# Three residual halves taken to the next product without TensorE, in a two-block fp32 kernel on one core

## Chip, core and metric
One core of one Trainium2 chip runs the whole program as one launch. The metric is device time in microseconds. The kernel before takes 901.46 us (median of 3 runs, 901.18 to 901.63).

## The reference
Batch 1, 256 tokens (two tiles of 128), model width 1024, all in fp32. Two blocks of two layers each follow one another on the same residual stream h:

```python
def first_block(x, p, ...):                # layer 0: gated linear attention, layer 1: differential attention
    for i in range(2):
        h = h + mixer_i(rms_norm(h, norm_mix[i]))
        h = h + swiglu(rms_norm(h, norm_ffn[i]), ffn_w_in[i], ffn_w_out[i])
        gate = jax.nn.sigmoid(rms_norm(h, ple_norm[i]) @ ple_w_gate[i])      # "the gate"
        h = h + gate * (p[i] @ ple_w_proj[i])
def diff_attn_mixer(h, ...):
    q, k, v = split(h @ w_in)              # each 256 x 1024, 8 heads of 2 x 64
    q, k = rope(rms_norm(q) * g_q), rope(rms_norm(k) * g_k)
    lam = exp(sum(lam_q1 * lam_k1)) - exp(sum(lam_q2 * lam_k2)) + lambda_init
    a = softmax(q0 k0 / 8) - lam * softmax(q1 k1 / 8)
    return (rms_norm(a @ v) * (1 - lambda_init)) @ w_out
def second_block(x, ...):                  # a short convolution layer, then block attention
```

Every normalised h is the left side of a large product, so it is needed transposed (features on the partitions), while the residual h is kept with tokens on the partitions.

## The kernel before
**Products.** All weights come as 296 units of 512 KB (256 rows by 512 columns), in the order of use, through a ring of four raw buffers; units are numbered 1 to 296 in program order, and END[tile] is the first unit of a tile. For each unit SP issues the transfer (it waits until VectorE's split of unit n - 3 is done, w_lo), ScalarE copies it rounded (whi, L671, fp32r), VectorE subtracts to get the rest (wlo, L1079), both in a ring of eight, and TensorE runs 12 matmuls of 512 columns (L1801): high by high, high by low and low by high, for two token tiles. A tile of 512 output columns is 4 units (11 for the second feed-forward product, 1 for the projection of p) and gathers in a pair of PSUM banks, 0/1 for even tiles and 2/3 for odd ones.

**Order on the engines.** Every queue is written out by hand. `split_to(end)` on ScalarE and VectorE works through all weight units below `end` before it goes on; AHEAD is 6. In differential attention the lists of DF_ORDER say after which unit step each piece of head work comes: an entry (u, step, arg) on ScalarE is preceded by `split_to(END[DF_IN] + u + 7)`, on VectorE by `split_to(END[DF_IN] + u + 6)`. On TensorE it stands before unit END[DF_IN] + u. The first units are 99 (gate of layer 0, PLE0), 109 (DF_IN), 207 (PLE1), 217 (CV_IN) and 257 (MB_IN).

**How the left sides are made.** Half of h (512 features) becomes ready a tile before the other. There are two ways:
- By TensorE: `h_T(1, version)` waits for the residual, and transposes eight 128x128 blocks into banks 6 and 7 (L1854); ScalarE scales and rounds them (`lhs_hi`, L682), VectorE makes the low part (`lhs_lo`, L1095). The second half goes this way at the gate of both layers (a hook before the tile's second unit) and at differential attention (the step "second", before unit 110).
- By VectorE and transfers: `second_blk` (L1119) transposes 32x32 blocks inside partitions into h_blk, SP writes them to DRAM and reads them back with the blocks in place (`second_blocks`, L499 and L502), `second_hi` (L704) and `second_lo` (L1133) make the two parts. Both feed-forward layers, the convolution and block attention take their second half so, and the gate's own output its first half (`gate_blocks`, L512, L515, L876, L1414). Before a wait SP first issues the weight transfers up to a fixed unit.

Where a second half comes by transfers, `first_tiles` interleaves the first two tiles in the order PAIR_ORDER, so that four units need the first half alone.

**Around the gate.** `ffn` on TensorE does tile 24 (4 units), then tile 25 (the projection of p, 1 unit), then 26 and 27. ScalarE takes the sigmoid of the gate's banks (L867), VectorE multiplies by the projection (L1396) and adds to h (L1400).

**Start of differential attention.** ScalarE squares a tile of q or k (L749, df_sq) and evacuates it (L737, df_tok). VectorE sums the squares (L1460), GpSimd makes the factors (L599), VectorE rotates (`df_rope`, L1484 to L1490) and, for tiles 1 and 2, multiplies by the factor (L1467). TensorE transposes the result (`df_T`, L2100), ScalarE copies it (L906), TensorE makes the scores (L2114). The rotation tables df_rot (L1439 to L1443) and the two sums for lambda are made by VectorE after the feed-forward part of layer 0 has ended, the exponentials of the sums by ScalarE (L948), and lambda by VectorE (L1495, L1497), all before the first split of this stage.

## Time and profile before

| | |
|---|---|
| median of 3 runs | 901.46 us |
| profiled execution | 900.89 us |
| its span, first to last instruction | 898.7 us |
| TensorE busy | 892.9 us, 4364 matmuls |
| VectorE busy | 654.6 us |
| ScalarE busy | 506.1 us |
| GpSimd busy | 63.4 us |
| moved by DMA | 187.47 MB, mean 209 GB/s |
| granted TensorE clock | full in all 40 slices |

The profiled execution's own time is 2.2 us longer than its span: what lies before the first instruction and after the last. A row of the timeline gives start, length, engine, line and operation, output <- inputs, how many instructions were merged, and in brackets how long the engine had been idle and what released it. Line numbers are those of the kernel printed above; `bank` is a PSUM bank.

### The profile page before, as it was taken

The page shows a single profiled execution, that of the slowest core. Times are in us where ns is not written, and L with a number is a line of the kernel's source. Part 1 is how long each engine was busy: PE and PEld are TensorE (multiplying, and loading weights), DVE is VectorE, ACT ScalarE, POOL GpSimd, SP SyncE. Part 2 cuts the span into 40 slices and gives each one's busy share as a digit, 9 for nine tenths or more (in the row PEclk, how much of TensorE's full clock was granted, in tenths as well). Part 3 has the DMA queues.
Part 4 walks back from the last instruction along what each step waited for, and adds up shares of the span by engine and source line. Part 5 has one row for each costly group of instructions (what it writes and reads, how often), then busy time and mean ns, then how long its engine had stood idle before and what let it go on. Part 6 is the DMA issues. An engine that isn't in the chain of part 4 may idle for free.

```text
span 898.7 us, 12238 instructions
## 1 busy us (share of the span) xinstructions
PE 892.9 (99%) x4364; PEld 737.0 (82%) x4364; DVE 654.6 (73%) x997; ACT 506.1 (56%) x820; POOL 63.4 (7%) x75
## 2 busy tenths in 40 slices
PE   9999999999999999999999999999999999999998
PEld 8988888888888888778888888888888888887777
DVE  6985478777735699997787776646679897779764
ACT  6756555444444667688564444435664544587681
POOL 0001000000000003211100000000010000215100
PEclk9999999999999999999999999999999999999999
DMA  7674458766755655424487667746568775656621
GB/s 271 197 240 143 162 189 301 277 242 243 240 194 194 227 199 201 160 97 141 139 284 265 237 239 246 254 142 231 202 220 278 260 253 192 207 200 234 227 70 47
DMA packets 76988, 187.47 MB, mean 209 GB/s; under 512 B 6852, under 2 KB 31812, under 8 KB 76936
## 3 DMA queue, kind: packets, MB, share of 16 engines
q1 hardware_dynamic: 75480, 182.99, 59.6%
q0 software_dynamic: 1024, 3.15, 1.0%
q10 hardware_dynamic: 432, 0.66, 0.2%
q8 instruction: 31, 0.51, 0.2%
q14 instruction: 21, 0.17, 0.1%
HBM read 171.83 MB, written 14.94 MB: 208 GB/s over the span
## 4 chain that ended last, share of the span: by engine, by line
PE 95%; DMA 2%; issue 2%; DVE 1%; POOL 1%; ACT 0%; DVEq 0%; POOLq 0%
PE bank L1801 84%; PE bank L1839 3%; PE bank L1854 1%; PE bank L2114 1%; PE bank L2140 1%; DMA mb_pT<-mb_blocks 1%; DMA mb_blocks<-p_tok 1%; DMA h<-x_dram 0%; PE bank L2224 0%; PE bank L2125 0%; PE bank L2253 0%; PE bank L1961 0%; PE bank L2009 0%; PE bank L2013 0%; PE bank L2100 0%
## 5 line engine op out<-in xcount | busy, mean ns | idle before, releaser
L671 ACT ACTIVATE whi<-raw 128x1024 fp32r<-128x1024 f32 x295 | 306.2, 1060 | 186.3 <-DMA raw<-stream_dram 108.8
L1079 DVE TENSOR_TENSOR wlo<-raw,whi 128x1024 fp32r<-128x1024 f32 x295 | 347.5, 1213 | 55.6 <-ACT whi L671 54.8
L1801 PE MATMUL bank<-whi,x_hi 128*128 128x512 f32 x560 | 152.5, 394 | 0.0
L1801 PE MATMUL bank<-wlo,x_hi 128*128 128x512 f32 x560 | 149.9, 389 | 0.0
L1801 PE MATMUL bank<-whi,x_lo 128*128 128x512 f32 x560 | 149.8, 389 | 0.0
L1801 PEld LDWEIGHTS bank<-wlo,x_hi 128*128 128x128 f32 x560 | 105.1, 188 | 22.3
L1801 PEld LDWEIGHTS bank<-whi,x_lo 128*128 128x128 f32 x560 | 105.1, 188 | 22.0
L1801 PEld LDWEIGHTS bank<-whi,x_hi 128*128 128x128 f32 x560 | 103.4, 188 | 21.7 <-issue 1.2
L1801 PE MATMUL bank<-whi,y_hi 128*128 128x512 f32 x396 | 108.0, 394 | 0.1
L1801 PE MATMUL bank<-wlo,y_hi 128*128 128x512 f32 x396 | 106.0, 390 | 0.0
L1801 PE MATMUL bank<-whi,y_lo 128*128 128x512 f32 x396 | 106.0, 389 | 0.0
L1801 PEld LDWEIGHTS bank<-wlo,y_hi 128*128 128x128 f32 x396 | 74.3, 188 | 15.7
L1801 PEld LDWEIGHTS bank<-whi,y_lo 128*128 128x128 f32 x396 | 74.3, 188 | 15.7
L1801 PEld LDWEIGHTS bank<-whi,y_hi 128*128 128x128 f32 x396 | 72.8, 188 | 16.0 <-issue 0.8
L824 ACT ACTIVATE ffn_silu<-bank,rstd 128x256 f32<-128x256 f32 x44 | 18.4, 471 | 76.8 <-PE bank L1801 76.8
L1303 DVE SCALAR_TENSOR_TENSOR ffn_mid<-bank,rstd,ffn_silu 128x256 f32<-128x256 f32 x44 | 19.3, 479 | 54.0 <-ACT ffn_silu L824 54.0
L1801 PE MATMUL bank<-whi,mid_hi 128*128 128x512 f32 x176 | 47.0, 389 | 0.0
L1801 PE MATMUL bank<-wlo,mid_hi 128*128 128x512 f32 x176 | 47.0, 389 | 0.0
L1801 PE MATMUL bank<-whi,mid_lo 128*128 128x512 f32 x176 | 47.0, 389 | 0.0
L1109 DVE TENSOR_TENSOR h<-h,bank 128x512 f32<-128x512 f32 x22 | 14.1, 683 | 44.7 <-PE bank L1801 44.5
L579 POOL TENSOR_TENSOR ms<-stats 128x2 f32<-128x2 f32 x8 | 4.9, 611 | 577.1 <-ACT junk L718 577.1
L1801 PEld LDWEIGHTS bank<-wlo,mid_hi 128*128 128x128 f32 x176 | 33.0, 188 | 6.9
(251 smaller groups left out, 891.4 us busy)
## 6 DMA issues: line engine op xcount, KB each, us to landing
raw<-stream_dram SPq DMA_DIRECT2D x295, 512.0 KB, 4.6
ffn_blocks<-ffn_blk SPq DMA_DIRECT2D x22, 256.0 KB, 2.0
ffn_land<-ffn_blocks SPq DMA_DIRECT2D x22, 256.0 KB, 3.7
second_blocks<-h_blk SPq DMA_DIRECT2D x8, 256.0 KB, 2.0
h_land<-second_blocks SPq DMA_DIRECT2D x8, 256.0 KB, 3.1
cv_blocks<-cv_blk SPq DMA_DIRECT2D x7, 256.0 KB, 5.2
cv_land<-cv_blocks SPq DMA_DIRECT2D x7, 256.0 KB, 3.3
h_blocks<-h_blk SPq DMA_DIRECT2D x3, 512.0 KB, 6.3
```

The source lines that it names most:

```text
L579: step(nc.gpsimd.tensor_tensor(ms[:, j, 0, :], stats[:, j, 0, :], stats[:, j, 1, :], ALU.add))
L671: A(whi[:, u % RING, :], raw[:, u % RAW, :], ACT.Copy).then_inc(sem("w_hi"), 1)
L824: A(sg[:, (t - tin) % 2, k, :], bank[2 * (t % 2) + k][:, 0:256], ACT.Silu, scale=rstd[:, j, k:k + 1]).then_inc(sem("ffn_silu"), 1)
L1079: V.tensor_tensor(wlo[:, u % RING, :], raw[:, u % RAW, :], whi[:, u % RING, :].bitcast(F32), ALU.subtract).then_inc(sem("w_lo"), 1)
L1109: V.tensor_tensor(h[:, t, half * HALF:(half + 1) * HALF], h[:, t, half * HALF:(half + 1) * HALF], bank[2 * (tile % 2) + t][:, :], ALU.add) ...
L1303: V.scalar_tensor_tensor(mid[:, (t - tin) % 2, :, k, :], bank[2 * (t % 2) + k][:, 256:512].rearrange("p (k n) -> p k n", k=2), rstd[:, j, ...
L1801: last = T.matmul(bank[pair + t][:, :], lhs[a][:, kt, t * P:(t + 1) * P], w[:, u % RING, kk * NW:(kk + 1) * NW], start=part != 1 and k == ...
L1839: last = T.matmul(bank[pair + hd // 2][:, hd % 2 * SEQ:(hd % 2 + 1) * SEQ], w[:, u % RING, kk * NW + hd * P:kk * NW + (hd + 1) * P], lhs[a ...
L1854: last = T.transpose(bank[b][:, k * SEQ + t * P:k * SEQ + (t + 1) * P], src[:, t, kt * P:(kt + 1) * P], ident)
L2114: last = T.matmul(bank[DF_S_BANKS[hd][m]][:, q * SEQ:(q + 1) * SEQ], dT[r, 0, hd, q * P:(q + 1) * P], dT[r, 1, hd, :], start=True, stop=True)
L2140: last = T.matmul(bank[b][:, q * SEQ + (hd % 2) * P:q * SEQ + (hd % 2 + 1) * P], daT[:, hd % 4, k * SEQ + q * P:k * SEQ + (q + 1) * P], dv ...
```

## The change
1. The second half of h at the gate (both layers) and at differential attention goes by VectorE and transfers; `h_T(1, ...)` is used nowhere.
2. The transfers of `second_blocks` and `gate_blocks` no longer go through DRAM. `cross` issues four of them, each from 32 partitions of h_blk to one quarter of h_land's free dimension.
3. The gate's units run in the order GATE_ORDER: gate, gate, projection, gate, gate. The next gate tile gathers in banks 4 and 5.
4. Differential attention's first two tiles run in PAIR_ORDER, by `first_tiles`; its lists change at the start: ScalarE takes tile 0 at step 6 (was 4), VectorE rotates it at 7 (was 5), TensorE transposes its first half at 11 (was 8).
5. The rotation tables and the two sums for lambda are made in `ffn(0)`, behind the gate's second half; ScalarE's exponential comes before the first Exp of the scores, VectorE's lambda before the first soft step. The tile df_rot lies elsewhere in memory.
6. Counters are named by a list of uses instead of numbers.

```diff
-PAIRED = (FFN_IN0, FFN_IN1, CV_IN, MB_IN)
+PAIRED = (FFN_IN0, DF_IN, FFN_IN1, CV_IN, MB_IN)
+USES = ("mix0", "ple0", "gate0", "df", "mix1", "ple1", "gate1", "cv", "mb")
+GATE_ORDER = ((0, 0), (0, 1), (1, 0), (0, 2), (0, 3))
 DF_ORDER = {
     "pe": (
-        (1, "second", 0), (8, "qkT", 0), (11, "qkT", 1), (12, "qkT", 2), (13, "scores", 0), (13, "qkT", 3),
+        (11, "qkT", 0), (11, "qkT", 1), (12, "qkT", 2), (13, "scores", 0), (13, "qkT", 3),
     "act": (
-        (4, "tile", 0), (8, "tile", 1), (9, "qkT", 0), (12, "qkT", 1), (12, "tile", 2), (12, "qkT", 2),
+        (6, "tile", 0), (8, "tile", 1), (11, "qkT", 0), (11, "qkT", 1), (12, "tile", 2), (12, "qkT", 2),
     "dve": (
-        (5, "rope", 0), (6, "more", 0), (6, "sums", 0), (8, "rope", 1), (8, "sums", 1), (10, "more", 1),
+        (7, "rope", 0), (7, "sums", 0), (8, "more", 0), (8, "rope", 1), (8, "sums", 1), (10, "more", 1),
...
+            def cross(dst, src, signal):
+                for i in range(P // B):
+                    sp.dma_start(dst[:, i, :], src[i * B:(i + 1) * B, :]).then_inc(sem(signal), 16)
             def second_blocks(r, tile):
-                at = END[tile] + (7 if tile == CV_IN else 8)
+                at = END[tile] + (7 if tile in (DF_IN, CV_IN) else 8)
                 fetch(done, at)
                 for q in range(2):
                     sp.wait_ge(sem("g_blk"), 2 * r + q + 1)
-                    sp.dma_start(s_dram[s, q], sblk[:, q, :]).then_inc(sem(f"g_out{q}"), 16)
-                for q in range(2):
-                    sp.wait_ge(sem(f"g_out{q}"), 16 * (r + 1))
-                    sp.dma_start(sland[:, q, :, :], s_dram[s, q]...).then_inc(sem(f"g_land{q}"), 16)
+                    cross(sland[:, q, :, :], sblk[:, q, :], f"g_land{q}")
...
                 done = half_blocks(n, tin + FT)
+                done = second_blocks(use(f"ple{n}"), tin + FT + 2)
                 done = gate_blocks(n, tin + FT + 2)
+                if n == 0:
+                    done = second_blocks(use("df"), DF_IN)
...
# ScalarE, ffn
                 split_to(END[tple] + 1 + AHEAD)
-                lhs_hi(src, norm_gain(j), (6, 7))
                 squares(j, 1)
+                second_hi(j, src, use(f"ple{n}"), END[tple])
                 for half in range(2):
                     t = tple + 2 * half
-                    split_to(END[t + 1] + AHEAD - 2 * half)
-                    c.wait(act, "w_used", END[t + 1])
+                    over = END[t + 1 + (half == 0)]
+                    split_to(over + AHEAD - 1 - half)
+                    c.wait(act, "w_used", over)
...
# VectorE, ffn
                 residual(tout + 1, 1)
-                split_to(END[tout + 2] + 1 + AHEAD)
-                lhs_lo(src, norm_gain(j), (6, 7))
+                second_blk(12 * n + 6)
+                second_lo(j, src, use(f"ple{n}"), END[tple])
+                if n == 0:
+                    df_tables()
...
-                    elif n == 0:
-                        split_to(END[DF_IN] + 1 + AHEAD)
-                        lhs_lo(dst, norm_gain(j + 1), (6, 7))
                     else:
                         second_blk(12 * n + 10)
-                        second_lo(j + 1, dst, 4, END[CV_IN] - 1)
+                        second_lo(j + 1, dst, use("cv" if n else "df"), END[tple + 4] - 1)
...
# TensorE
-                product(tple, src, "ple_sig", need=more2, hooks=[(1, second_half2)])
-                product(tple + 1, PT, "ple_gated", need=[("pT", 2 * (n + 1))])
-                product(tple + 2, src, "ple_sig")
+                more2 = list(half0) + second_need(use(f"ple{n}"))
+                for at, (t, k) in enumerate(GATE_ORDER):
+                    product(tple + t, PT if t else src, "ple_gated" if t else "ple_sig" if k == 3 else None,
+                            need=[("pT", 2 * (n + 1))] if t else more2, only=k, at=END[tple] + at)
+                product(tple + 2, src, "ple_sig", pair=4)
...
-            product(DF_IN, Y, "df_in", need=df_half0, beside=df_beside)
-            for t in range(1, 6):
+            first_tiles(DF_IN, Y, "df_in", list(half) + second_need(use("df")), df_beside)
+            for t in range(2, 6):
                 product(DF_IN + t, Y, "df_in", beside=df_beside)
```

`df_tables` holds the table and sum operations of L1439 to L1451 unchanged, except that the products of the lambda vectors are written to df_m2 and no longer to df_o.

## Rows read from the trace of the kernel before

**Rows 1.** the page, busy shares (part 1) and head of the chain (part 4).
```profile
PE 892.9 (99%) x4364; PEld 737.0 (82%) x4364; DVE 654.6 (73%) x997; ACT 506.1 (56%) x820; POOL 63.4 (7%) x75
...
PE 95%; DMA 2%; issue 2%; DVE 1%; POOL 1%; ACT 0%; DVEq 0%; POOLq 0%
```
**Rows 2.** the chain that ended last, in order of time: start us, us, what.
```profile
117.41 184.98 PE bank L1801 x816
302.39 0.87 PE bank L1854 x8
303.26 27.34 PE bank L1801 x120
330.61 0.90 PE bank L1854 x8
...
362.53 0.28 issue
362.81 0.63 PE bank L2100 x4
...
627.67 116.98 PE bank L1801 x516
```
**Rows 3.** timeline, gate: start us, us, engine, line, operation, tiles, count [idle before <-releaser].
```profile
299.70 1.28 DVE L1109 TENSOR_TENSOR h<-h,bank 128x512 f32<-128x512 f32 x2 [2.73 <-PE bank L1801]
...
311.48 1.27 ACT L867 ACTIVATE ple_gate<-bank,rstd 128x512 f32<-128x512 f32 x2
```
**Rows 4.** timeline, start of the convolution layer: VectorE, ScalarE, SP.
```profile
652.27 1.29 DVE L1396 TENSOR_TENSOR ple_gated<-ple_gate,bank 128x512 f32<-128x512 f32 x2 [1.90 <-PE bank L1801]
...
654.68 2.22 DVE L1119 STREAM_TRANSPOSE h_blk<-h 128x256 f32<-128x256 f32 x4
...
661.32 1.15 DVE L1133 SCALAR_TENSOR_TENSOR x_lo<-h_land,cols,x_hi 128x128 fp32r<-128x128 f32 x4
...
660.57 0.91 ACT L704 ACTIVATE x_hi<-h_land,cols 128x256 fp32r<-128x256 f32 x2 [2.13 <-DMA h_land<-second_blocks]
...
663.96 1.06 ACT L671 ACTIVATE whi<-raw 128x1024 fp32r<-128x1024 f32 x1 [0.39 <-issue]
665.64 1.06 ACT L671 ACTIVATE whi<-raw 128x1024 fp32r<-128x1024 f32 x1 [0.61 <-DMA raw<-stream_dram]
...
659.37 17.23 SPq L438 DMA_DIRECT2D raw<-stream_dram  x9
```
**Rows 5.** all uses of tile h_land: issue of one read (ns), its landing (us).
```profile
L502 SPq DMA_DIRECT2D h_land<-second_blocks x8: 370/371/371, 124.6 to 767.8; - x8
...
DMA to landing us min/median/max: 2.6/3.2/4.9
```
**Rows 6.** all uses of tile h_blk: landing of its writes to DRAM.
```profile
DMA to landing us min/median/max: 2.0/2.0/6.4
```
**Rows 7.** timeline, start of differential attention: VectorE, ScalarE.
```profile
336.39 0.28 DVE L1439 SCALAR_TENSOR_TENSOR df_rot<-consts,rows 128x128 f32<-128x128 f32 x1
...
340.18 4.63 DVE L1079 TENSOR_TENSOR wlo<-raw,whi 128x1024 fp32r<-128x1024 f32 x4 [0.57 <-ACT whi L671]
344.72 0.75 DVE L1484 TENSOR_TENSOR df_m<-df_tok,df_rot 128x256 f32<-128x256 f32 x2
...
361.42 1.29 DVE L1467 TENSOR_TENSOR df_tok<-df_tok,df_ss 128x512 f32<-128x512 f32 x2
...
334.13 1.28 ACT L948 ACT_TABLE_LOAD   x1
...
339.03 3.89 ACT L671 ACTIVATE whi<-raw 128x1024 fp32r<-128x1024 f32 x4
342.82 1.24 ACT L749 ACTIVATE df_sq<-bank,rstd 128x512 f32<-128x512 f32 x2
...
347.28 1.06 ACT L671 ACTIVATE whi<-raw 128x1024 fp32r<-128x1024 f32 x1 [1.11 <-DMA raw<-stream_dram]
```
**Rows 8.** tile raw, 330 to 366 us: issue to landing of blocks.
```profile
DMA to landing us min/median/max: 3.1/4.4/4.8
```

More of the change, by code:

```diff
@@ L431, in _ @@
                     SOURCE[END[tile] + n] = END[tile] + (KT // 2) * t + k
+            for tile in (PLE0, PLE1):
+                for n, (t, k) in enumerate(GATE_ORDER):
+                    SOURCE[END[tile] + n] = END[tile + t] + k
             SOURCE[END[CV_OUT] + 3], SOURCE[END[CV_OUT] + 4] = END[CV_OUT] + 4, END[CV_OUT] + 3
@@ L510, in gate_blocks @@
                 for t in range(TT):
-                    sp.wait_ge(sem("g_blk"), 2 * (2 * n + 1) + t + 1)
-                    sp.dma_start(g_dram[n, t], gblk[:, t, :]).then_inc(sem(f"g_out{t}"), 16)
-                for t in range(TT):
-                    sp.wait_ge(sem(f"g_out{t}"), 16 * (2 * n + 2))
-                    sp.dma_start(gland[:, t, :, :], g_dram[n, t].rearrange("q n -> (q n)")
-                                 .rearrange("(i p w) -> p i w", i=P // B, p=P)).then_inc(sem(f"g_land{t}"), 16)
+                    sp.wait_ge(sem("g_blk"), 2 * use(f"gate{n}") + t + 1)
+                    cross(gland[:, t, :, :], gblk[:, t, :], f"g_land{t}")
                 return max(done, at)
@@ L528, in _ @@
                 done = END[out_tile]
-                done = second_blocks(2 * n, tin)
+                done = second_blocks(use(f"mix{n}"), tin)
                 fetch(done, done_at(tin) + 10)
@@ L550, in _ @@
             done = max(done, END[MB_IN])
-            done = second_blocks(5, MB_IN)
+            done = second_blocks(use("mb"), MB_IN)
             fetch(done, UNITS)
@@ L694, in mixer_lhs @@
                 squares(j, 1)
-                second_hi(j, dst, 2 * (j - 1) // 3, END[out + 4])
+                second_hi(j, dst, use(f"mix{(j - 1) // 3}"), END[out + 4])
             def second_hi(j, dst, r, base):
@@ L729, in next_lhs @@
                 squares(j, 1)
-                second_hi(j, dst, 5, END[first + 1])
+                second_hi(j, dst, use("mb"), END[first + 1])
             def evacuate(tile, j, dst, width, signal, func=ACT.Copy, scale=None):
@@ L955, in _ @@
                 elif step == "scores":
+                    if arg == 0:
+                        act.wait_ge(sem("df_lam"), 2)
+                        A(lam[:, 2:4], lam[:, 0:2], ACT.Exp).then_inc(sem("df_lamexp"), 1)
                     df_exp(arg)
@@ L1753, in product @@
             def product(tile, lhs, signal, kt0=0, need=None, hooks=(), beside=None, part=None,
-                        only=None, at=None, turned=False, inside=None):
-                pair = 2 * (tile % 2)
+                        only=None, at=None, turned=False, inside=None, pair=None):
+                pair = 2 * (tile % 2) if pair is None else pair
                 hooks = dict(hooks)
@@ L2143, in df_av @@
                 last.then_inc(sem("df_av"), 1)
-            df_half0, df_pairs = list(half) + [None, None], [None] * 4
+            df_pairs = [None] * 4
             def df_beside(u):
@@ L2150, in df_beside @@
                         continue
-                    if step == "second":
-                        df_half0[2:4] = h_T(1, 3)
-                    elif step == "qkT":
+                    if step == "qkT":
                         df_T(arg)
```

98 lines of the change are left out of this document (45 added, 53 removed).

## The prediction
> **What bounds the kernel now.** First the page's busy shares and the head of its chain [rows 1]: TensorE is busy 99% of the span and the chain that ended last is TensorE for 95%. So only two things can move the time: matmuls taken out, and new waits of TensorE. Then the chain in order of time [rows 2]. A unit is 12 matmuls of one 512 KB weight block; 184.98 us for 68 units is 2.72 us each, back to back. Three pieces of eight transposes (L1854) stand in that stream before units 100, 110 and 208: 0.87, 0.90 and 0.87 us (the third, at 626.80, repeats the first). These are the second residual halves that the change takes from TensorE. The one wait in this stretch is 0.28 us, before the transposes of head step 2 at 362.81. Third, the other engines around these places: VectorE and ScalarE in the gate [rows 3] and in differential attention [rows 7], and, as a model of what the change puts there, the start of the convolution layer, which already gets its second half by VectorE and transfers [rows 4].
>
> **Removed.** 24 transposes, 0.87 + 0.90 + 0.87 = 2.64 us, all on the path. With nothing added the profiled execution goes from 900.89 us (span 898.7) to 898.25; the median of the runs shown, 901.46, lies 0.57 above the profiled one, and I carry differences over to it: 898.8.
>
> **The gate's second half (twice).** Unit 98 ends at 302.39 - 2.72 = 299.67. With the projection's unit in third place, TensorE wants the second half at unit 102, 3 x 2.72 later, 307.83. VectorE adds the residual 299.70 to 300.98 [rows 3]; four block transposes take 2.2 us, the first pair being ready after 1.15 [rows 4], so SP starts at 302.1 (300.98 + 1.15). It issues four transfers at 0.37 us each [rows 5], the last at 303.2 to 303.5. The trace has no transfer from SBUF to SBUF. Nearest rows: 2.0 us to DRAM in the median (6.4 for the one form of 512 KB) [rows 6], back from it 2.6 to 3.2 and at most 4.9 [rows 5]. With 3.2 the half lands at 306.7, ScalarE scales two tiles in 0.91, 307.6: 0.2 us to spare. With 2.0 there are 1.4 to spare, with 4.9 TensorE waits 1.5 us, twice in the kernel. The lower parts: VectorE does the residual, the transposes (to 303.2), four weight splits (to 307.9), then 1.15 to 309.1; TensorE wants them two thirds into unit 102, 309.6. I take no wait, between ends of 0 and 3.0 for both.
>
> The Trainium skill ("DMA: Bandwidth & Descriptors", Anatomy of one DMA) gives a fixed cost of about 2.0 us, most of it the receipt from the target memory, heaviest for HBM; by it a direct 64 KB transfer lands some 2.15 us after issue, an estimate from that page, and the case with 4.9 has less to speak for it. The trace agrees in that 256 KB go in 2.0 us.
>
> **The tables made earlier.** Twelve small products and the lambda sums, 336.39 to 338.89, 2.5 us of VectorE [rows 7], now come after the gate's second half, at 310.3 to 312.8, then one weight split to 314.0. TensorE ends unit 103 in the new kernel at 299.67 + 5 x 2.72 = 313.3, and ScalarE's first sigmoid (0.63, half of the pair's 1.27 [rows 3]) at 313.95. VectorE is there at the same moment: no cost. Weights are split up to unit 107 by then, four units ahead of TensorE. The gate's first half then lands no later than before (its transfers save a round trip), so unit 109 finds it.
>
> **Differential attention's second half.** Unit 108 ends 0.87 us earlier than before, at 303.26 + 9 x 2.72 - 0.87 = 326.9. The convolution's start has the same structure, and TensorE waits for nothing there [rows 2]; I carry its offsets over [rows 4], counted from the first gated product (652.27 there, 326.9 here). VectorE's transposes end at +4.6 (331.5), four splits (units 112 to 115) at +9.1 (336.0), the lower parts at +11.4 (338.3) if it never waits. TensorE wants the half at unit 113, 337.8, the lower parts at 339.6. No wait here.
>
> **What follows it: the new order of the head steps.** Here I expect the loss. Before, ScalarE evacuates tile 0 after the splits up to unit 119 and VectorE rotates it after them; the new lists put these at steps 6 and 7, after the splits up to unit 121. Those two splits must come first in both queues, and they come round a ring of four raw buffers: VectorE's split n lets SP fetch unit n+4, which lands 4.4 us later in the median (3.1 to 4.8), ScalarE rounds it in 1.06, VectorE subtracts in 1.16 [rows 7, 8].
> - SP has issued the eight direct transfers by 326.9 + 3.6 (the first pair of block transposes) + 8 x 0.37 = 333.5, then fetches 116. In the convolution the first unit after SP was free (659.37) was rounded at +4.6, the next at +6.3 [rows 4]. So unit 116 at 338.1 and 117 at 339.8, VectorE done with them at 340.4 and 342.1 (with the hand-over between the engines). Before the change all four had landed long before they were wanted, because both engines were held by the lambda chain until 339.03 [rows 7].
> - Unit 121's fetch is freed by 117's split: 342.1 + 4.4 = 346.5, rounded at 347.6. Only now does ScalarE take tile 0: squares 1.24, first token half 0.63, rotation can start at 349.4 (before: 344.72, with TensorE 1.8 us later in its stream).
> - Tile 2 wants tile 0's banks at unit 117, 326.9 + 8 x 2.72 = 348.7; they are free at 350.1. That is a new wait of 1.4 us, contained in the next.
> - VectorE from the first rotation to the last unit factor: before 344.72 to 362.71 with five splits (units 120 to 124), 18.0 us without a gap [rows 7]. Now three splits: 18.0 - 2 x 1.16 = 15.7. 349.4 + 15.7 = 365.1, and TensorE's transposes of step 2 at 365.2 instead of 362.81: +2.4.
> From there the order is the old one, and ScalarE's copy behind these transposes is late with them, so TensorE carries +2.4 through the stage. It has already used the two gains of 0.87 and 0.90. The last 0.87 (before unit 208) remains: +2.4 - 0.9 = **+1.5 us**.
>
> Bounds of this term. Low: VectorE goes on at 338.3 and never waits; its nine splits, rotations, sums and factors are 9 x 1.16 + (18.0 - 5 x 1.16) = 22.6 us, ending at 360.9, TensorE's wait is about the old 0.28 and the whole change gives -2.6. With every landing at its minimum of 3.1 us, tile 0 is taken at 345.3 and the step comes at 362.9: -0.8 overall. High: fetches at 4.8 behind each other put tile 0 at 348.5: +2.4.
>
> **Small edits.** The two small lambda operations on VectorE move from before the first split of rows 7 (338.89 to 340.18, mostly waiting) into the first soft step, and the Exp table load of 1.28 us, which ran at 334.13 in a gap [rows 7], comes before the first Exp. Both then stand between the first scores and TensorE's first aT transposes, three units (8.2 us) later by the lists; I take 0, between 0 and the load's 1.3. Layer starts that used DRAM before (four) had no wait and keep none; there the change saves traffic only. The projection's banks: the gate's second tile moves to banks 4 and 5, free for long: 0.
>
> **Rivals.**
> - *Full gain.* Weights land early, VectorE has no gap, the order costs nothing: -2.4 to -2.6 us, 898.9. For it: VectorE is relieved of 2.5 us there. Against: in rows 7 a unit's rounding waits 1.11 us for its landing (two more such waits follow), with the queue fed no worse than it will be.
> - *Short delay.* The same chain with quick landings: between -0.9 and +0.7 us, near 901.3.
> - *The direct transfers are late* (slower for certain): four small transfers and the raw blocks share one queue, landing at 4.9 as the slowest read did. Its place is unit 102 and unit 210; it decides once a landing takes over 3.4 us from the last issue. 2 x 1.5 on top of +1.5 (part of the first is absorbed, since the attention chain starts later by the same): +2.4 to +4.5, 904.6. The Trainium skill ("DMA: Bandwidth & Descriptors", Issuing engines are not separate DMA queues) says that all DMAs run on the same 16 engines and interleave; in the convolution's start a weight block issued at 659.7 was rounded only at 665.64 [rows 4], which agrees.
>
> **How the numbers follow.** The forecast's case (tile 0 taken between 346.8 and 348.5) holds from +0.7 to +2.4 us: 0.42; short delay 0.20; full gain 0.22; late transfers 0.16. A change of under 0.2%, 1.8 us, can't be told from none here. Of the first case a third lies over 1.8 (0.14), so slower is 0.14 + 0.16 = 0.30, faster 0.22, same 0.28 + 0.20 = 0.48. Time of the likeliest: 901.46 + 1.5 = 902.96, given as 902.9. The range holds the full gain nearly whole and half of the late transfers: 898.9 to 904.7; the forecast's own case is 902.2 to 903.9.
>
> **What would show it.** Right: no L1854 pieces before units 100, 110, 208; a wait of TensorE at unit 117 for df_tok (L737) of 1 to 2 us and one before L2100 of 2 to 4; tile 0 squared (L749) at 347 or 348; whi waits for raw ahead of it. Wrong: tile 0 squared by 344, or L2100 without a wait (full gain); a wait of TensorE near 307 to 310 for x_hi or x_lo (late transfers); a wait before aT (the table load is not hidden).

## The result and the profile after

The changed kernel takes 906.54 us (median of 7 runs, 905.33 to 908.03), the kernel before 901.46 (median of 7 on the same chip, 900.16 to 904.4): ratio 1.0058, 95% interval 1.0046 to 1.0069, so 5.1 us slower. The forecast was 902.9, between 898.9 and 904.7: the sign was right, the size was not (slower had been given 0.30). The profiled execution took 905.53 us (span 903.7), before 900.89 (898.7).

The page of the kernel after, busy shares, head of the chain, and the issues of the direct transfers (KB each, us to landing):
```profile
PE 891.9 (99%) x4340; PEld 735.3 (81%) x4340; DVE 663.7 (73%) x1021; ACT 508.1 (56%) x820; POOL 65.7 (7%) x75
...
PE 88%; DVE 4%; DMA 3%; SPq 2%; issue 1%; ACT 1%; ACTq 0%; DVEq 0%
...
h_land<-h_blk SPq DMA_DIRECT2D x72, 64.0 KB, 2.1
```
Against [rows 1]: 24 instructions fewer on TensorE, 24 more on VectorE with 9.1 us of work. TensorE's share of the chain falls from 95 to 88%. That is not the length of its waits, which are 7.4 us in the four lines below and under 1% of the span: where TensorE waits, the chain runs back through VectorE, SP and the transfers that it waited for, while TensorE was still busy. Where it waits, the list of TensorE's waits after says (us in total, times, longest):
```profile
PE bank L1810 <- ACT df_tok L745: 4.5, 1, 4.5
PE bank L2106 <- issue: 1.6, 1, 1.6
...
PE bank L1810 <- ACT x_hi L885: 0.7, 1, 0.7
PE bank L1810 <- ACT y_hi L712: 0.6, 1, 0.6
```
The first two stand in differential attention's start, where [rows 2] had 0.28. Timeline of that stretch after, in turn for SP, ScalarE and VectorE (columns as in rows 3):
```profile
318.72 5.08 SPq L504 DMA_DIRECT2D h_land<-h_blk  x8
...
330.88 5.22 SPq L504 DMA_DIRECT2D h_land<-h_blk  x8
336.50 6.34 SPq L460 DMA_DIRECT2D raw<-stream_dram  x5
...
337.63 0.91 ACT L712 ACTIVATE y_hi<-h_land,cols 128x256 fp32r<-128x256 f32 x2 [1.67 <-DMA h_land<-h_blk]
339.89 1.06 ACT L679 ACTIVATE whi<-raw 128x1024 fp32r<-128x1024 f32 x1 [1.34 <-DMA raw<-stream_dram]
342.51 1.06 ACT L679 ACTIVATE whi<-raw 128x1024 fp32r<-128x1024 f32 x1 [1.56 <-DMA raw<-stream_dram]
344.52 1.06 ACT L679 ACTIVATE whi<-raw 128x1024 fp32r<-128x1024 f32 x1 [0.95 <-DMA raw<-stream_dram]
...
350.34 1.25 ACT L757 ACTIVATE df_sq<-bank,rstd 128x512 f32<-128x512 f32 x2
...
341.08 1.23 DVE L1086 TENSOR_TENSOR wlo<-raw,whi 128x1024 fp32r<-128x1024 f32 x1 [1.76 <-ACT whi L679]
...
352.20 0.76 DVE L1492 TENSOR_TENSOR df_m<-df_tok,df_rot 128x256 f32<-128x256 f32 x2 [0.51 <-ACT df_tok L745]
...
366.64 1.29 DVE L1475 TENSOR_TENSOR df_tok<-df_tok,df_ss 128x512 f32<-128x512 f32 x2
```
SP is in the eight issues from 330.88 to 336.10 and only then fetches unit 116, whose buffer VectorE had freed near 333.0 (the first of its four splits from 331.83). Unit 116 lands 3.4 us after its issue; the three blocks sent close behind it (337.5 to 338.6) take 5.0 to 7.1 us, where [rows 8] had 4.8 at most. Every rounding up to the one before tile 0 waits for its raw block; tile 0 is squared at 350.34, where [rows 7] has 342.82. The same in windows of 4 us (busy us and count of PE, PEld, DVE, ACT, POOL; granted clock; DMA share; GB/s):
```profile
334.00:338.00 4.00, 4.00 (x20) 3.30 (x18) 3.46 (x7) 2.02 (x6) 2.50 (x3) 1.00 0.45 109
338.00:342.00 4.00, 4.00 (x19) 3.34 (x18) 2.06 (x5) 1.60 (x3) 0.00 (x0) 1.00 0.95 306
342.00:346.00 4.00, 4.00 (x20) 3.30 (x19) 1.92 (x3) 2.36 (x3) 0.00 (x0) 1.00 0.82 323
...
352.00:356.00 4.00, 3.16 (x8) 2.51 (x9) 3.73 (x7) 3.50 (x6) 0.90 (x1) 0.59 0.71 267
356.00:360.00 4.00, 4.00 (x19) 3.29 (x18) 3.90 (x8) 3.45 (x5) 2.58 (x2) 0.99 0.41 133
```
The DMA engines are half idle while SP is held, then loaded at 0.95 and 0.82 to refill the ring, and VectorE has 2 us of work in 4. From 352 us on, behind the first rotation, VectorE is full (3.73 and 3.90 of 4). TensorE itself, timeline after:
```profile
347.29 1.07 PE L1810 MATMUL bank<-whi,y_lo 128*128 128x512 f32 x4
352.84 2.04 PE L1810 MATMUL bank<-whi,y_hi 128*128 128x512 f32 x4 [4.49 <-ACT df_tok L745]
354.69 1.74 PE L1810 MATMUL bank<-wlo,y_hi 128*128 128x512 f32 x4
...
357.19 1.09 PE L1810 MATMUL bank<-whi,y_hi 128*128 128x512 f32 x4
...
368.04 0.63 PE L2106 MATMUL bank<-consts,df_tok 128*128 128x128 f32 x4 [1.61 <-issue]
...
371.35 1.14 PE L2120 MATMUL bank<-df_qkT 64*128 64x256 f32 x8
```
Groups of four matmuls that take 1.07 us elsewhere take 2.04 and 1.74 behind the wait, at a granted clock of 0.59 over the window of 4 us, which mixes 1.2 and 2.4 GHz. The next unit comes 4.35 us later (352.84 to 357.19); a unit behind a wait with the clock at 1.00 took 2.84 (e18 below).

Two marks that all kernels share measure the place: the first matmul of unit 99 (the gate) and the first score matmul. Before they are 66.65 us apart (299.50, 366.15), after 72.13 (299.22, 371.35): +5.48. It adds up: waits 4.49 + 1.61 - 0.28, clock 1.51, less two pieces of transposes (0.87 + 0.90) = 5.56. Outside this stretch: -0.28 ahead of it; the third piece gone (-0.87) with waits of 0.6 and 0.7 in the second gate and the convolution's start; waits of 1.1 us in block attention that the trace of before has and this one has not. That makes 4.5 of the span's 5.0; where the other 0.5 lies stays open.

### The profile page after: what moved, and what is told of

The parts are those of the page before. It is cut to its first block, busy times and chain, and to the rows that moved or that the text cites. A ratio compares the mean times of both kernels' runs of the same rounds, so it can differ in the third digit from the quotient of the medians.

```text
span 903.7 us, 12249 instructions
## 1 busy us (share of the span) xinstructions
PE 891.9 (99%) x4340; PEld 735.3 (81%) x4340; DVE 663.7 (73%) x1021; ACT 508.1 (56%) x820; POOL 65.7 (7%) x75
## 4 chain that ended last, share of the span: by engine, by line
PE 88%; DVE 4%; DMA 3%; SPq 2%; issue 1%; ACT 1%; ACTq 0%; DVEq 0%
PE bank L1810 77%; PE bank L1848 3%; DMA raw<-stream_dram 2%; SPq L504 2%; DVE wlo L1086 1%; PE bank L2120 1%; PE bank L1863 1%; PE bank L2146 1%; PE bank L2228 1%; PE bank L2257 1%; PE bank L2131 0%; DVE h_blk L1126 0%; DMA h_land<-h_blk 0%; DVE ple_gated L1431 0%; PE bank L1906 0%
## 5 line engine op out<-in xcount | busy, mean ns | idle before, releaser
L1810 PEld LDWEIGHTS bank<-whi,y_lo 128*128 128x128 f32 x396 | 74.4, 188 | 15.7
L1810 PEld LDWEIGHTS bank<-whi,mid_hi 128*128 128x128 f32 x176 | 33.0, 188 | 6.9
```

Of the source, the lines that this page charges most:

```text
L1810: last = T.matmul(bank[pair + t][:, :], lhs[a][:, kt, t * P:(t + 1) * P], w[:, u % RING, kk * NW:(kk + 1) * NW], start=part != 1 and k == ...
```

## The experiments

"Stage" is the distance between the two marks in the run's one profile; ratios are timed, against the kernel before on the same chip. e7 is not in the table: its kernel is longer by design and ran once (926.45 us).

| run | what it is | ratio [95%] | stage, us (before 66.65) | longest waits of TensorE in it |
|---|---|---|---|---|
| after | the change | 1.0058 [1.0046, 1.0069] | 72.13 | 4.49, 1.61 |
| e1 | through DRAM | 1.0059 [1.0043, 1.0075] | 69.97 | 2.07, 1.54 |
| e2 | old order of head steps | 1.0065 [1.0053, 1.0077] | 73.03 | 0.99, 5.44 |
| e6 | both (the base below) | 1.0054 [1.0041, 1.0067] | 71.65 | 4.59 |
| e14 | attention's half alone, direct | 1.0060 [1.0043, 1.0077] | 71.49 | 2.25, 1.55 |
| e3 | gate's half alone, direct | 1.0013 [1.0002, 1.0023] | 67.52 | 1.44 |
| e8 | gate's half alone, DRAM | 0.9991 [0.9982, 1.0000] | 65.44 | none |
| e17 | e8, tables at the old place | 0.9990 [0.9979, 1.0000] | 65.89 | 0.33 |
| e4 | before, direct transfers | 0.9999 [0.9990, 1.0007] | 66.66 | 0.30 |
| e13 | before, tables early | 1.0011 [1.0002, 1.0020] | 66.89 | 0.47 |
| e9 | after, issued by GpSimd | 1.0133 [1.0118, 1.0149] | 73.40 | 2.96, 1.65 |
| e10 | e9, old order | 1.0096 [1.0081, 1.0110] | 72.95 | 3.45, 1.28 |
| e11 | e6, unit 116 fetched first | 1.0040 [1.0027, 1.0053] | 70.43 | 0.97, 2.88 |
| e12 | e6 less VectorE's lower parts | 1.0056 [1.0043, 1.0069] | 71.77 | 4.43 |
| e15 | e6 less VectorE's transposes | 1.0042 [1.0026, 1.0059] | 71.68 | 4.38 |
| e16 | e6, splits before the half | 1.0076 [1.0055, 1.0098] | 77.48 | 4.60, 2.87 |
| e18 | before + a wait at unit 117 | 1.0037 [1.0024, 1.0050] | 67.07 | 0.66 |
| e19 | before + a longer one | 1.0083 [1.0065, 1.0101] | 71.21 | 3.25 |

**Is it the transfers or the order of the head steps? (e1, e2, e6)** e1 sends the halves through DRAM as before, e2 puts head step "tile 0" back to step 4 and its rotation to 5, e6 does both:
```diff
-                    cross(sland[:, q, :, :], sblk[:, q, :], f"g_land{q}")
+                    sp.dma_start(s_dram[r, q], sblk[:, q, :])...
+                for q in range(2):
+                    sp.wait_ge(sem(f"g_out{q}"), 16 * (r + 1))
+                    sp.dma_start(sland[:, q, :, :], s_dram[r, q]...)
...
-        (6, "tile", 0), (8, "tile", 1), (11, "qkT", 0),
+        (4, "tile", 0), (8, "tile", 1), (11, "qkT", 0),
```


> The changed kernel with its block transfers through DRAM again (one write and one read for each half, as before the change), all else as changed. Theory A (SP's issue): each of the 8 direct transfers costs SP 0.60 us of issue, so SP fetches unit 116 only at 336.5; with the round trip SP is free 3.5 us after the first pair of blocks, at 334.4, 2.1 us earlier. Then tile 0 is taken 2.1 us earlier, TensorE's wait at unit 117 falls from 4.5 to about 2.4 us, the waits at units 210 and 217 (0.6 and 0.7) go, and the time falls by 3.4 to 5 us, to 901.5 to 903. Theory B (the order of the head steps alone): the direct transfers cost nothing, the time stays at 906 within 1 us or rises, since the round trip lands the halves later.

> The changed kernel with the first head steps where they were: ScalarE takes tile 0 at step 4 (was 6), VectorE rotates at 5 and 6 (was 7 and 8); direct transfers kept. Theory A (SP's issue feeds the weights late, the order is second): ScalarE takes tile 0 at 346.8 instead of 350.3, the wait at unit 117 falls from 4.5 to about 1.1 us and TensorE's clock does not fall, but VectorE's chain is still fed late and ends at 366.6 instead of 367.9: 1.3 us faster, 905.2. Theory B (order alone): the whole loss of the attention stage goes, 5 us or more faster, 901 or less.

> The changed kernel with both: block transfers through DRAM and the first head steps where they were. Theory A: SP free 2.1 us earlier and tile 0 taken before the splits of units 120 and 121: VectorE's first rotation at 346.5, its chain ends at 364.5, 3.5 us before the changed kernel's, and the gate's waits go: 901.7, so still no faster than the kernel before. Theory B (order alone): as the early order alone, 901 or less. If the two costs add up fully (2.1 and 5 us): 899.


All three lie at the changed kernel's time (906.3, 906.3 and 906.1 us), so the gains expected by theory A for e1 and e6 and by theory B for e2 and e6 did not come. e2's waits of TensorE:
```profile
PE bank L2106 <- DVE df_tok L1475: 5.4, 1, 5.4
...
PE bank L1810 <- ACT df_tok L745: 1.0, 1, 1.0
```
The order moves the wait and does not make it: the 4.5 us stood at unit 117, now 5.4 stand at step 2. The step that I blamed in the prediction is not the cause. The new order even shields something: with it the slow clock behind the first wait falls into time that TensorE would have spent in the second (step 2 comes at 368.04 and the scores 3.31 us later); in e2 step 2 comes at 367.70 and the scores at 372.68, 4.98 us later. e1's profile has the best stage of the three: SP fetches unit 116 there 35.06 us after unit 99 begins, 37.28 in the changed kernel, and the stage is 2.16 us shorter. Its timed runs do not show it; they reach from 903.7 to 908.8, so that gain is open.

**Which part? (e3, e8, e14, e4, e13, e17)** e3 and e8 undo differential attention's part (TensorE transposes the half, old order) and keep the gate's; e14 undoes the gate's and keeps the other; e4 and e13 put one edit into the kernel before; e17 is e8 with tables and lambda where they were.
```diff
-PAIRED = (FFN_IN0, DF_IN, FFN_IN1, CV_IN, MB_IN)
+PAIRED = (FFN_IN0, FFN_IN1, CV_IN, MB_IN)
...
-                second_hi(j + 1, X if n else Y, use("cv" if n else "df"), END[tple + 4] - 1)
+                if n == 0:
+                    lhs_hi(Y, norm_gain(j + 1), (6, 7))
```


> The changed kernel with differential attention's second half, unit order and lists as before the change (eight transposes on TensorE, no interleaved tiles); the gate's second halves by VectorE and direct transfers, the gate's unit order and the early tables stay. Theory A: the loss sits in the attention stage; here two groups of transposes are gone (1.8 us) against waits of 1.3 us at units 210 and 217: 901.0, the time before within 1 us. Rival (the gate's direct transfers are the larger loss): 903 or more.

> The kernel whose gate alone is changed (two groups of transposes gone, early tables), with its block transfers through DRAM. With direct transfers it took 901.83, with waits of 0.4 and 1.4 us before and behind unit 110. Theory A: SP is held 3.5 us instead of 5.1 at the gate, so the waits shrink by 1 to 1.5 us and the time is 900 to 901, a little under the kernel before. Rival (the gate's second half by VectorE is late by VectorE's and ScalarE's own work, not by SP): 901.8 or more.

> The changed kernel with the gate's part undone (its second half by TensorE's transposes again, its tiles in their old order); differential attention's half, the direct transfers, the new order of head steps and the early tables stay. Theory A (nearly all of the loss is differential attention's half): TensorE loses 16 of the 24 transposes less of work, about 0.9 us gained in place of 2.6, and has the same wait of 4 to 5 us ahead of unit 117 or the scores with the clock at half behind it: 905.5 to 907, ratio 1.0045 to 1.0065. Theory B (the gate's part, by holding SyncE just before, makes half of the loss): 903 to 904.5, ratio 1.002 to 1.0035, and the wait is 2 us shorter.

> The kernel before with one part of the change: the block transfers that it already had (four second halves, two gate outputs) go directly instead of through DRAM, four issues for each pair. Theory A: the weights come later at these places too, but there is slack in the feed-forward and convolution layers; at the gate SP is held 5.1 us instead of 4.1: within 1 us of 901.05. Rival (issue time counts everywhere): 903 or more.

> The kernel before with one part of the change alone: VectorE makes the rotary tables and lambda's sums ahead of the gate's second half, and lambda is finished at its new place; all transposes, transfers and the order of head steps are those of before. VectorE is relieved of some 2 us in the stage that starts differential attention. Theory 1: the wait of 0.28 us at the unit before the scores goes and nothing else changes: 901.0 to 901.3, ratio 0.9990 to 1.0005. Theory 2 (the tables, made while the gate runs, hold the gate's halves): a wait at the gate's second half of the units appears, ratio above 1.001.

> The gate's part alone through DRAM (900.2, ratio 0.9991 when it was run before) and the tables and lambda made at their old place. The tables made early, alone, were at ratio 1.0011. Theory A (tables made early hold the gate's products of VectorE for a little): without them the gate's part gives 0.3 to 1 us more: 899.3 to 900, ratio 0.998 to 0.9985. Theory B (they cost nothing, 1.0011 was the noise of a measurement): 900.2 again, with the 0.28 us wait at the unit before the scores back: ratio 0.9987 to 0.9997.


Differential attention's half alone is the whole loss: e14's ratio is the changed kernel's. Its waits:
```profile
PE bank L1805 <- ACT df_tok L741: 2.2, 1, 2.2
PE bank L2104 <- issue: 1.6, 1, 1.6
```
The gate's half is worth about 0.9 us through DRAM (e8, e17: two runs that agree, though each interval reaches 1.0000). Direct, it is not: e3 and e8 differ by 2.2 in a thousand with intervals apart, though the same transfers at the old places cost nothing (e4). e3 fetches the weights of the next stage from 324.91, e8 from 322.55, and TensorE waits 1.44 us at 335.9. Tables made early are not worth moving: e13 has the 0.28 us wait gone and one of 0.47 at 314.65 in its place, and is 1.1 in a thousand slower; e17 and e8, with the gate's new order, are equal.

**What does the issue cost? (e7, e9, e10)** e7 is the kernel before with groups of transfers behind its end, all queues empty; e9 and e10 let GpSimd issue all direct transfers.
```diff
+            for i in range(4):
+                sp.dma_start(land0[:, i, :], h[i * B:(i + 1) * B, 0, 0:NW])...
+            sp.wait_ge(sem("out_done"), 16 * (5 + 4))
...
+                for i in range(P // B):
+                    nc.gpsimd.dma_start(dst[:, q, i, :], src[i * B:(i + 1) * B, q, :])...
```


> The kernel before with nothing changed but its last microseconds: there SyncE issues, each group waited for before the next, four transfers of 32 x 512 float from SBUF into a tile of 128 x 4 x 128 (the shape of the direct transfers), four of 32 x 512 into the same shape in SBUF, four of 32 x 512 to DRAM, four from DRAM as 128 x 128, and then four single ones of 128 x 512 in SBUF. Theory 1 (the issue pays for how the bytes are laid out on the receiving side): the first group costs 0.55 to 0.60 us per issue as in the changed kernel, the second 0.33 to 0.38. Theory 2 (the issue pays for SBUF on both sides): both cost 0.55 or more, the DRAM ones 0.33 to 0.38. Theory 3 (the issue was long because the queue was full of weights then): all are under 0.4 here, where the queues are empty. The time as a whole is longer by the transfers added at the end (10 to 15 us) and says nothing.

> The changed kernel with all its direct block transfers issued and waited for by GpSimd, which is idle there, each before the row norm of the same place; SP does weight blocks alone. Theory A (SP, held for 3.5 to 5 us by each set of waits and issues, feeds the weights late): SP fetches unit 116 at 333.0, as soon as its buffer is free, instead of 336.5; tile 0 is taken about 3 us earlier, the wait at unit 117 falls from 4.5 to 1 to 1.5 us, TensorE's clock stays up (1.6 us), and the gate's waits go if GpSimd's transfers land in time: 901 to 903. Theory C (VectorE's own work bounds the stage: four block transposes and the later splits; the feed does not matter): 905 to 906.5, with VectorE without gaps from 338 to 366.

> As the kernel with GpSimd's transfers, and the first head steps where they were before the change (tile 0 at step 4, rotation at 5 and 6). Theory A: with both the feed and the order mended VectorE's chain ends at about 362, TensorE waits under 1 us: 899 to 901. Theory C: as the other early orders, 905 to 906.


The lines of e7's groups (issue in ns, min/median/max): SBUF to 128x128 slices, SBUF to the same shape, SBUF to DRAM, DRAM to 128x128, and 128x512 in SBUF:
```profile
L563 SPq DMA_DIRECT2D raw<-h x4: 595/604/696, 899.6 to 901.6; - x4
...
L566 SPq DMA_DIRECT2D raw<-h x4: 591/592/603, 903.7 to 905.6; - x4
...
L569 SPq DMA_DIRECT2D h_blocks<-h x4: 342/420/431, 907.7 to 909.0; - x4
...
L572 SPq DMA_DIRECT2D raw<-h_blocks x4: 588/602/604, 910.7 to 912.6; - x4
...
L576 SPq DMA_DIRECT2D raw<-h x4: 465/484/517, 914.9 to 922.0; - x4
```
0.60 us also with empty queues, so theory 3 falls; the layout at the receiver makes no difference (first against second group), so theory 1 falls; and the fourth group comes from DRAM at 0.60, so theory 2 does not hold as I put it. What is common to the three dear groups is that a quarter of a tile (64 KB) goes to SBUF; the rule behind it stays open. Their landing is 2.0 to 2.5 us. GpSimd is no way out: e9 took 912.6 and e10 910.2 us where 901 to 903 and 899 to 901 were expected. The issues themselves are not late: the eight for this stage take 4.32 us (333.90 to 338.22) and start when VectorE's first pair of transposes is ready. The landings are. The page of e9 (KB each, us to landing), against 2.1 us from SP in the changed kernel's page above:
```profile
h_land<-h_blk POOLq DMA_DIRECT2D x72, 64.0 KB, 3.5
```
In this stage they took 2.0 to 4.6 us (2.1 to 2.3 from SP), at the first gate 2.1 to 4.7. TensorE waits for the halves in both gates (1.65 us at 309.63 in e9), and in the stage ScalarE, which takes the half before the next weights, stands 3.47 us for its second pair. SP was free there and fetched unit 116 at 335.94, as soon as its buffer was, and TensorE still waited 2.96 us at unit 117: freeing SP alone does not help when the half comes late. Whether the landings are long because of GpSimd's issue or because SP's weight blocks are then under way beside them was not tested.

**What makes tile 0 late? (e11, e12, e15, e16)** All from e6. e11 fetches unit 116 between SP's writes and reads of the half; e12 leaves out VectorE's lower parts of that half (2.2 us of work), e15 its four transposes (the transfers carry what was there); e16 has VectorE split two units first and SP fetch two units more before the half.
```diff
+                if r == use("df"):                                   # e11
+                    fetch(at, at + 1)
...
+                            last = V.memset(dm2[:, 0, ...], 0.0)     # e12
...
+                                V.memset(sblk[:, q, 0:4], 0.0)...    # e15
...
+                            split_to(END[tple + 4] + 5)              # e16
```


> The changed kernel with its transfers through DRAM and its old order of head steps (906.1, ratio 1.0054, when it was run before), and one edit more: SyncE fetches unit 116 (its weights' two halves) between the DRAM writes and the DRAM reads of differential attention's second half, in place of after both. Theory A (the weights come late to the rounding, so that ScalarE and after it VectorE stand idle: rounding waited 2.17 us and VectorE 2.34 us there): the raw tile comes about 2 us earlier, tile 0's splits start at about 339.9 in place of 341.9, TensorE's wait ahead of the scores (4.6 us) goes to under 3 and the clock's share of the loss with it: 903.5 to 905, ratio 1.002 to 1.004. Theory B (VectorE has too much to do in this stage, whenever it is fed): the same time as without the edit, ratio 1.0045 to 1.0065, and VectorE's idle time only moves.

> The same base (transfers through DRAM, old order of head steps; 906.1, ratio 1.0054), and differential attention's second half leaves out VectorE's lower parts (h - bf16(h), four instructions for each tile, 2.2 us in all), with four tiny memsets in their place: this part of the computation is left out, so that its time is read as that of 2.2 us less work on VectorE. Theory A (VectorE waits for the weights there, not for itself): no change, ratio 1.0045 to 1.0065, VectorE idle for 4.5 us in place of 2.3 before its splits. Theory B (VectorE's work is what is too long): the scores start 2.2 us earlier, TensorE's wait falls from 4.6 to 2.4 and the clock's loss by half: 902.5 to 904, ratio 1.001 to 1.003.

> The changed kernel with transfers through DRAM and the old order of head steps (906.1, ratio 1.0054), and VectorE's four transposes of differential attention's second half left out (two tiny memsets stand for them; the transfers carry what the buffer held): this part of the computation is left out. Theory A (the 2.2 us of transposes ahead of the four splits that free the raw buffers make the weights late): splits, fetches and transfers all come 2.1 us earlier, the scores too, TensorE's wait falls from 4.6 to about 2.5 and the clock's loss becomes smaller: 903 to 904, ratio 1.002 to 1.003. Theory B (SyncE's wait for the round trip is what holds): the raws come earlier by as much only because the transfers do, so A and B part in the next run and not here; a result at 906 would make both wrong.

> The same base, nothing left out: VectorE makes two of the four splits before its transposes, and SyncE fetches two units more (116 and 117) before it takes up the transfers. Theory A: the raws of 116 and 117 are fetched at about 332.5 and 333.7 in place of 335.2 and 335.7, tile 0's chain starts about 2.5 us earlier; differential attention's half lands about 2.3 us later, and TensorE waits some 2 us for it at unit 113, which costs nothing so long as the scores are what it waits for later: the waits are split in two of 2 to 2.5 us, the scores come 1.5 to 2.5 us earlier, 903.5 to 905, ratio 1.0025 to 1.004. Theory B (the round trip alone holds the weights, and behind the new place it holds the next ones): 906 or more, ratio over 1.005.


VectorE's work ahead of the rotation is not it. Without 2.2 us of it (e12), and without 2.1 us at another place (e15), the stage stays within 0.15 us of e6's. e15's SP and ScalarE:
```profile
329.98 0.80 SPq L513 DMA_DIRECT2D second_blocks<-h_blk  x2
333.67 1.02 SPq L516 DMA_DIRECT2D h_land<-second_blocks  x2
335.05 16.02 SPq L461 DMA_DIRECT2D raw<-stream_dram  x9
...
338.63 0.91 ACT L721 ACTIVATE y_hi<-h_land,cols 128x256 fp32r<-128x256 f32 x2 [1.26 <-DMA h_land<-second_blocks]
339.98 1.06 ACT L688 ACTIVATE whi<-raw 128x1024 fp32r<-128x1024 f32 x1 [0.44 <-DMA raw<-stream_dram]
```
The writes start as soon as they can, and unit 116 is still fetched at 335.05 (335.20 in e6): SP stands 2.9 us between writes and reads (330.78 to 333.67). So in that run the round trip holds it, not the transposes; my theory A for e15 fell. None of these runs takes work from VectorE behind the first rotation, where it has no gap: from there to step 2 it takes 18.1 us in the kernel before and in e6, and 15.7 in the changed kernel with two splits fewer. So step 2 is late by what tile 0 is late; whether less work in that stretch would bring it forward was not tried. e11 takes that hold away for one unit:
```profile
332.14 1.37 SPq L513 DMA_DIRECT2D second_blocks<-h_blk  x2
334.29 0.33 SPq L448 DMA_DIRECT2D raw<-stream_dram  x1
334.75 0.96 SPq L519 DMA_DIRECT2D h_land<-second_blocks  x2
...
338.77 1.85 ACT L724 ACTIVATE y_hi<-h_land,cols 128x256 fp32r<-128x256 f32 x4 [2.38 <-DMA h_land<-second_blocks]
340.52 1.05 ACT L691 ACTIVATE whi<-raw 128x1024 fp32r<-128x1024 f32 x1
```
The block has landed when ScalarE comes to it (no wait at 340.52), but the half, now behind it, lands later, and ScalarE takes the half first: tile 0 is squared 45.53 us after unit 99 begins, against 45.89 in e6. The stage gains 1.2 us, of which 0.9 is less slow clock, as part of the wait moved to unit 113 (0.97). Timed it is 903.94, as theory A had it, two us under e6, but with intervals that overlap. e16 drives the exchange further and loses: the half, written at 334.95, is rounded at 342.36, and TensorE waits 4.60 us for it at unit 113 and 2.87 at step 2. Its expectation (903.5 to 905) missed by 4 us: I had not counted that the two units fetched ahead delay both legs of the round trip.

**What does such a wait cost? (e18, e19)** The kernel before, where TensorE waits at unit 117 for one or two GpSimd powers that start when unit 116 is done.
```diff
+            pool.wait_ge(sem("w_used"), END[DF_IN] + 8)
+            nc.gpsimd.tensor_tensor(idle[:, 8:16], idle[:, 0:8], neg_half[:, 0:8], ALU.pow)
+            nc.gpsimd.tensor_tensor(idle[:, 16:24], idle[:, 0:8], neg_half[:, 0:8], ALU.pow).then_inc(sem("gap"), 1)
...
+                    if u == END[DF_IN] + 8:
+                        pe.wait_ge(sem("gap"), 1)
```


> The kernel before, and TensorE is made to wait once ahead of unit 117, for one small GpSimd instruction (128 x 2 power, 1.05 us) that starts when unit 116 is done: a wait of about 1.4 us and nothing else. Theory A (a wait costs its length less the 0.28 us that TensorE waits later in the kernel before, and below 2 us the clock holds): the granted clock stays at 0.95 or more, +0.9 to +1.2 us: 902.2 to 902.6, ratio 1.001 to 1.0014. Theory B (any such wait costs clock): the clock of the next 4 us is near 0.6 and the time is 2.5 us or more above before, ratio over 1.0025.

> The same with two GpSimd instructions of 1.94 us: a wait of about 4.2 us. Theory A (a wait of this length costs its length less 0.28, and the clock at about 0.6 for some 4 us after it, 1.6 us more): +5 to +6 us: 906.3 to 907.4, ratio 1.0057 to 1.0067. Theory B (the low clock in the changed kernel had another cause): the clock stays at 1.0, +3.9: 905.1, ratio 1.004. A third possibility: what TensorE loses is partly given back downstream, where it had waited for VectorE or for a transfer (0.28 at the scores, 1.1 us later on): then 1 us less than either.


The powers took 0.69 us (e18) and 1.64 and 1.67 (e19) and not 1.05 and 1.94, so the waits are 0.66 and 3.25 us. TensorE in e19:
```profile
355.75 2.02 PE L1809 MATMUL bank<-whi,y_hi 128*128 128x512 f32 x4 [3.25 <-ACT whi L677]
357.57 1.84 PE L1809 MATMUL bank<-wlo,y_hi 128*128 128x512 f32 x4
359.25 1.09 PE L1809 MATMUL bank<-whi,y_lo 128*128 128x512 f32 x4
360.18 1.08 PE L1809 MATMUL bank<-whi,y_hi 128*128 128x512 f32 x4
```
From unit 109's first matmul to the scores: 38.54 us before, 38.85 in e18 (+0.31, the wait less 0.28), 43.09 in e19: +4.55 = 3.25 - 0.28 + 1.58. The unit behind the wait takes 4.43 us (355.75 to 360.18) against 2.84 in e18. So the wait by itself costs the clock, 1.6 us, in a kernel that has nothing else changed. The totals can't be used for that, and both lie above what was expected (905.19 for 902.2 to 902.6, 908.48 for 906.3 to 907.4): both kernels reach unit 99 already 1.5 to 2.0 us late and lose about 2 us once more in the second half. In each block's feed-forward part a stretch of 68 units takes 186.5 us in both where it took 185.0, with no wait and the clock at full. The cause of that stayed open.

## Why the prediction was wrong

- **Removed**, right: the pieces before units 100, 110 and 208 are gone. Unit 117 would have begun 2.05 us earlier in the trace after (348.2).
- **The gate's second half**, nearly right for the wrong reason: no wait at unit 102, 0.6 us at unit 210. Four issues were taken at 0.37 us each [rows 5], the read of a whole 256 KB tile; a half needs eight, a direct one takes 0.60 in the median, and eight take 5.1 to 5.3 (6.25 once, just at unit 210, where one issue held SP for 1.77). The half was there at 308.6 and not at 306.7. That cost nothing because unit 102 needs only its first pair (rounded 306.05 to 306.96, unit 102 at 307.38) and unit 103 the second; the prediction asked for all of it at unit 102. Landing, 2.1, was at the quick end of the bounds and the rival of late landings fell. The first sigmoid came at 314.49 (313.3 predicted). The gate is worth about 0.9 us by e8 and nothing directly (e3). "The gate's first half then lands no later than before" held at layer 0; at the convolution's start TensorE waits 0.73 us for it (x_hi, L885).
- **The tables made earlier**, right for this kernel: no measurable cost or gain (e17 against e8). In the kernel before, with the gate's old order, e13 shows a new wait of 0.47 us.
- **Differential attention's second half**: "No wait here" was right for TensorE, wrong for what matters: SP. It was carried over from the convolution's start, where SP is as much held [rows 4], but where no head step is queued behind the next weight splits.
- **The new order of the head steps**: this is the step that failed, in its first term. The chain was the right one (SP free, unit 116, 117, 121, tile 0, rotation, step 2) and its last link was exact: 15.7 us from the rotation's start to step 2's transposes; 352.20 to 367.93 is 15.73. But SP was free at 336.1 in place of 333.5: 2.3 us are the issues (5.22 in place of 8 x 0.37), 0.3 its start. Unit 116 was rounded at 339.89 (338.1), 117 at 342.51 (339.8), tile 0 squared at 350.34 (347.6), step 2 at 368.04 (365.2): SP's 2.6 us are 1.8 at unit 116, 2.7 at 117 (whose block took 5.0 us to land) and from there on 2.7 to 2.8 unchanged. And the name of the step is wrong: with the old order the loss is the same (e2, e6), as is e14's. This account rests on the trace. e1, where SP is free earlier, has step 2 earlier by 2.2 us in its profile, 0.7 us behind the predicted place, but not a shorter time; so that SP's issue time alone is the missing 2.8 us in the timed runs is not shown. Shown is that attention's half is the loss (e14) and that neither the order (e2) nor VectorE's work ahead of the rotation (e12, e15) makes it.
- **The clock**: no term. Its 1.5 us at unit 117 happened to fall inside the time up to step 2 and added nothing to the 2.8 there; in the old order (e2) it counts. e19 shows that a wait by itself brings it: 1.6 us behind a wait of 3.25. The Trainium skill ("TensorE: Matmul & The Clock Gate", HAM oscillation — how this bites in real kernels) warns that an idle TensorE is re-throttled and that the next work starts cold; e19's trace agrees.
- **Sum**: 2.8 of the 3.6 us missed are this one term. Of the other 0.8, the waits of 0.6 us in the second gate and 0.7 at the convolution's start (none was predicted), less the block attention's 1.1, make 0.2; the rest is the 0.5 of the profile that stayed open, and rounding.
- **Small edits**, right: no wait ahead of the first aT.

What held the gain back is therefore: TensorE gives 24 transposes (2.6 us) to a way that leads through SP and ScalarE in order, just where both must feed the ring for the next stage. At the gate it gains about 0.9 us through DRAM, at the edge of what the runs can tell, and at differential attention it costs 5 us. Both kinds of transfer hold SP by 2 to 3.5 us, and putting the weights first makes the half late. Whether a fifth raw buffer would free it was not tried.

The best kernel that was run is the gate's half alone through DRAM: 900.19 us (e8, ratio 0.9991) or 900.57 (e17, 0.9990), under 0.2% better than before.

## What to carry to other kernels

When work is moved from the bounding engine to "free" ones, add up what the issuing queue does between two fetches, with the issue time of that very shape of transfer, and follow the ring of buffers behind it; VectorE, with 2 us of work in 4, was idle because it was fed late, and giving it less work ahead of that place changed nothing. If a wait only changes its place when you reorder its consumers, look at the feed. A wait of TensorE of 2 us or more is to be priced with some 1.5 to 2.8 us of slow clock on top, unless a second wait follows that swallows it.

## What was not expected of the hardware

- Issuing a 64 KB transfer to SBUF on SP took 0.59 to 0.60 us from SBUF or DRAM (e7), one to DRAM 0.34 to 0.43, a 128x512 one within SBUF 0.48; whole 256 KB reads took 0.37 [rows 5]. From GpSimd it took 0.58 in the median (e9), and the landing 3.5 us in the median where SP's took 2.1.
- Behind TensorE waits of 0.66, 1.55 and 1.61 us the granted clock stayed at 1.00; behind 2.07 (e1), 2.25 (e14), 3.25 (e19) and 4.49 us (after) it fell, and the next unit took 4.38, 4.42, 4.43 and 4.35 us, against 2.84 at full clock. It is not always so cheap: behind 2.96 us (e9) and 4.60 us (e16) the next unit took 5.26 and 5.28. Behind waits at step 2 of 5.44, 4.59 and 4.38 us (e2, e6, e15) the scores came after 4.98, 5.80 and 6.11 us, against 3.34 in the kernel before. So the price was 1.5 to 2.8 us and did not grow with the wait's length.
- A GpSimd power of 128x8 took 1.64 us in e19 with nothing beside it on its queue, as did those of block attention in the kernel before (mean 1.64); those of differential attention took 1.94 in the mean there.
